# A two-layer hybrid encoder on one NeuronCore: the weight-only steps between the first projection's units stand one unit later

## What is computed

```python
h = layer_norm(x, ln_in_w, ln_in_b)
for l in range(DEPTH):                       # DEPTH = 2
    proj = h @ w_in[l]                       # 1024 -> 3088 columns
    p_ret, p_s5, p_hy, p_ml = split(proj)
    y = concat([retention(p_ret), s5(p_s5, ...), hyena(p_hy, filters), mlstm(p_ml)])
    h = layer_norm(DN_ALPHA * h + y @ w_out[l], ...)
    f = swiglu(h, ...) if l % 2 == 0 else moe_swiglu(h, ...)
    h = layer_norm(DN_ALPHA * h + f, ...)
```

## Time and profile before

| | us |
|---|---|
| median of 3 runs | 1953.71 (1953.68 to 1954.87) |
| the profiled execution, its own time | 1956.23 |
| its span, first to last instruction | 1954.4 |
| PE busy | 1762.7 (90% of the span) |
| DVE busy | 1360.3 (70%) |
| ACT busy | 951.5 (49%) |
| mean granted TensorE clock, share of 2.4 GHz | 0.907 |

### The profile page before, as it was taken

The page is one execution under the profiler, slowest core; times in us unless marked ns, Lnnn a source line. Parts: engine busy times, 40 slices in busy tenths (PEclk is TensorE's granted clock), DMA queues, the critical chain, the costliest instruction groups (busy, mean ns, idle before and its releaser), DMA issues.

```text
span 1954.4 us, 20243 instructions
## 1 busy us (share of the span) xinstructions
PE 1762.7 (90%) x7868; PEld 1396.0 (71%) x7868; DVE 1360.3 (70%) x1437; ACT 951.5 (49%) x951; POOL 54.0 (3%) x33
## 2 busy tenths in 40 slices
PE   6988697999979869789999899899899899998995
PEld 5556575888866658478778678778678687787784
DVE  3449845556621795468878688788688787787886
ACT  1240212445611011266666576666667666666763
POOL 0002100000000110000000000000000000000000
PEclk9996568999989765889999999999899999999997
DMA  9240033434642000748878788788688788787980
GB/s 407 81 172 1 1 133 118 186 138 166 244 193 99 31 1 0 297 182 350 348 284 346 281 343 333 311 348 342 269 350 347 307 341 323 298 347 283 361 324 23
DMA packets 42223, 454.80 MB, mean 233 GB/s; under 512 B 4496, under 2 KB 4624, under 8 KB 9360
## 3 DMA queue, kind: packets, MB, share of 16 engines
q1 hardware_dynamic: 39824, 445.03, 58.2%
q10 hardware_dynamic: 2304, 8.39, 1.1%
HBM read 443.96 MB, written 9.44 MB: 232 GB/s over the span
## 4 chain that ended last, share of the span: by engine, by line
PE 81%; DVE 11%; ACT 3%; issue 2%; DMA 2%; SPq 0%; DVEq 0%; POOL 0%; PEldq 0%
PE bank L908 30%; PE bank L928 15%; PE bank L818 6%; PE bank L543 4%; PE bank L552 4%; PE bank L749 3%; PE bank L827 3%; DVE ring_lo L1566 2%; PE bank L873 2%; PE bank L710 2%; PE bank L892 2%; ACT ex_up_hi L1105 2%; PE bank L683 1%; DMA cst<-const 1%; PE bank L916 1%
## 5 line engine op out<-in xcount | busy, mean ns | idle before, releaser
L1566 DVE TENSOR_TENSOR ring_lo<-ring,ex_up_hi 128x2048 fp32r<-128x2048 f32 x226 | 517.4, 2290 | 125.9 <-ACT ex_up_hi L1105 125.9
L1105 ACT ACTIVATE ex_up_hi<-ring 128x2048 fp32r<-128x2048 f32 x226 | 432.7, 1915 | 181.5 <-PE bank L908 167.8
L908 PE MATMUL bank<-ex_up_hi,ex_x_hi 128*128 128x512 f32 x896 | 371.4, 414 | 14.2 <-DVE ring_lo L1566 13.5
L908 PE MATMUL bank<-ring_lo,ex_x_hi 128*128 128x512 f32 x896 | 353.4, 394 | 5.8 <-issue 5.8
L908 PE MATMUL bank<-ex_up_hi,ex_x_lo 128*128 128x512 f32 x896 | 352.6, 394 | 0.0
L1686 DVE TENSOR_TENSOR ring_lo<-ring,ex_w_hi 128x2048 fp32r<-128x2048 f32 x112 | 255.6, 2282 | 0.0
L908 PEld LDWEIGHTS bank<-ex_up_hi,ex_x_hi 128*128 128x128 f32 x896 | 169.2, 189 | 63.3 <-DVE ring_lo L1566 19.6
L1190 ACT ACTIVATE ex_w_hi<-ring 128x2048 fp32r<-128x2048 f32 x112 | 213.2, 1904 | 0.0
L928 PE MATMUL bank<-ex_w_hi,ex_mid_hi 128*128 128x512 f32 x448 | 182.1, 407 | 34.3 <-DVE ex_mid_lo L1680 34.3
L908 PEld LDWEIGHTS bank<-ring_lo,ex_x_hi 128*128 128x128 f32 x896 | 168.7, 188 | 38.3
L908 PEld LDWEIGHTS bank<-ex_up_hi,ex_x_lo 128*128 128x128 f32 x896 | 169.3, 189 | 35.8 <-issue 3.8
(11 more groups left out here) (317 smaller groups left out, 2356.3 us busy)
## 6 DMA issues: line engine op xcount, KB each, us to landing
ring<-moe SPq DMA_DIRECT2D x113, 2048.0 KB, 7.7
ring<-moe SPq DMA_DIRECT2D x112, 1024.0 KB, 7.6
ring<-ffn SPq DMA_DIRECT2D x11, 3072.0 KB, 11.1
ring<-w_in SPq DMA_DIRECT2D x8, 3072.0 KB, 16.1
ring<-w_out SPq DMA_DIRECT2D x4, 2048.0 KB, 8.3
tab<-yT ACTq DMA_DIRECT2D x16, 512.0 KB, 2.7
ring<-tab SPq DMA_DIRECT2D x2, 3072.0 KB, 10.3
lnb<-ln SPq DMA_DIRECT2D x5, 1024.0 KB, 6.9
```

Of the source, the lines that this page charges most:

```text
L908: ins = mm(b[:, :], ex_x[j][x_][:, k, :], (ex_up_hi, lo)[w_][:, k, :], start=(k == 0 and m == 0), stop=(k == KT - 1 and m == 2))
L1105: act(ex_up_hi[:, HS * q:HS * (q + 1), :], wt[:, HS * q:HS * (q + 1), :], ACT.Copy).then_inc(e_uh, 1)
L1566: tt(ring_lo[s][:, half], ring[s][:, half], hi.bitcast(F32), ALU.subtract).then_inc(e_ul, 1)
```

## The change

The rows of `BESIDE` change, and nothing else:

```diff
-        BESIDE = [(0,), (1,), (2, 3), (4, 5, 6), (7, 8, 9), (10, 11), (12, 13), (14, 15), (16, 17), (18, 19), (20,),
+        BESIDE = [(), (0,), (1, 2), (3, 4, 5), (6, 7, 8), (9, 10), (11, 12), (13, 14), (15, 16), (17, 18), (19, 20),
                   (), ()]
```

## The result

The change makes the kernel slower: 1968.05 us median against 1956.35 (six runs each), ratio 1.0058, interval 1.0044 to 1.0072. That is 11.7 us where the forecast said 7.7. The time lies outside the stated range of 1956.0 to 1966.0. Two things make up the miss of 6.6 us against 1961.4: before itself has a median of 1956.35 in six runs, 2.6 above the 1953.71 of three on which the forecast was put, and the change costs 4.0 more than forecast. Taken as differences from 1953.71, the ends of the range are +2.3 and +12.3, and 11.7 lies near the upper one.

The account below looks back on a forecast made before the run. The last table store was taken to set the mixers' start, any shift reaching the end. Part 1's +2.1 and part 2's +5.6 gave +7.7 us on the median 1953.71, so 1961.4 us, range 1956.0 to 1966.0.

Parts of the forecast that it names:

- part 1: PE up to the end of unit 6: removed and added waits and slow clock balance to +2.1 us (-2.0 to +4.3).
- part 2: From unit 6 to the last table store: DVE row and two more tables make the load's issue 5.6 us later.
- The first rival, ACT drained in time: Behind unit 6: ACT again waits for unit 10, only one more table counts (2.82 us); 1958.6 us, chance 0.12.
- the second, waits that cost no clock: PE's new waits bring no slow clock: part 1 is -2.0, total +3.6 us, 1957.3, within 0.2%; chance 0.1.
- The faster one: Mixers get a better clock through their later start: -9.1 us, 1944.6, if the mean rose to 0.75; chance 0.05.
- The rival with all costs at their upper ends: Whole kernel: +4.3 + 5.6 + 2.1 = +12.0 us, 1965.7; chance 0.12.
- Unit 1 no longer stands behind the constants: PE at unit 1 and step 0: 3.36 idle, 2.25 and 0.44 slow clock removed, together 6.05 us gained.
- Step 2 behind step 1: PE waits for step 1's sine: 4.7 us idle plus 2.25 slow clock, 6.95 added.
- Step 5 behind step 3: PE waits for step 3's window product on DVE: 1.5 us idle added, clock cost taken as 0.
- Step 7 behind step 6: PE waits for DVE's four L1273: 1.9 us idle plus 1.80 slow clock, 3.7 added.
- Removed ahead of step 6: PE's old wait for step 5's window product goes: 2.21 us idle and 1.80 slow clock, 4.01 gained.
- 2.1 us for the mixers: Starting the mixers at another moment may move them by about 2.1 us either way.

Follow-up runs that it names:

- e4: Kernel before with step 20 alone moved one unit earlier, so all eight tables stand ahead of unit 10's reading out; ratio 0.9988, 2.2 us faster.
- e8: Kernel before with filler steps reordered: step 0 behind unit 1, dependent steps apart, step 11 early, all tables ahead of unit 10; ratio 0.9938, 1941.03 us.
- e2: Kernel before with the change's second half alone (steps 11 to 20 as in the change); ratio 1.0007, 1.4 us slower.
- e5: The unedited change again, beside new runs of before; ratio 1.0073, 14.3 us slower.
- e6: The change plus six unused matmuls of constants in two of PE's new waits (ahead of steps 2 and 5); ratio to before 0.9997.
- f1: Kernel before, unedited, profiled a second time; 1961.5 us.
- f3: Kernel before, unedited, profiled a third time; 1955.3 us.
- d04 to d16: Kernel before with 4, 8, 12 or 16 chained DVE products ahead of layer 0's first mixer tile; ratios to before 1.0003, 1.0019, 1.0032, 1.0040.
- e1: Kernel before with the change's first half alone (steps 0 to 10 as in the change, 11 to 20 as before); ratio 0.9999.
- f2: The kernel of e1 profiled a second time, no further edit; 1957.6 us.
- f4: The kernel of e1 profiled a third time, no further edit; 1967.4 us.
- e3: Kernel before with step 2 alone moved right behind step 1, after unit 1; ratio 1.0044, 8.6 us slower.
- e7: Kernel before with no step behind unit 0, early steps one unit later, dependent ones mostly apart, 12 to 20 unchanged; ratio 0.9975, 5.2 us faster.

## Why the prediction was wrong

The steps that failed are two terms of part 1: the 6.05 us to be gained at the constants, which is 4.1, and the 0 us of slow clock behind step 5's wait, which is 1.8 with its matmul. Together they are 3.8 of the 5.0 us by which part 1 came out dearer than the 2.1 forecast. The kinds of cost (waits, and slow matmuls behind them) and part 2 were right.

**Read right.** The mixers' start hangs on the last table store (e4, e8). Behind unit 6 the row of rotation, step 11, step 12 and rotation puts the first table 14.8 us behind it, ACT no longer waits for unit 10, and two tables follow it: +5.7 measured in after, e2, e5 and e6, +5.6 forecast. The first rival, ACT drained in time, is out, and so is the second, waits that cost no clock. The faster one is out too: both kernels' mixers lie between 168 and 173 us. The rival with all costs at their upper ends (1965.7) comes nearest to the time, but not by its terms: part 1 is above its upper end, and the mixers in after gave nothing (168.4 against 170.1).

**Wrong: part 1, "+2.1 us at the end of unit 6".** Nine executions with before's order up to unit 6 (before, f1, f3, e2, e4, d04 to d16) have the rotation at 88.6 to 92.9, mean 90.5. Five with the change's order (after, e5, e1, f2, f4) have it at 96.0 to 98.2, mean 97.6. The part costs 7.1 us, above the upper end of 4.3 that I gave it. The one profile that I read has the latest rotation of the nine, and against it alone the cost is 4.8. With 5.7 the 7.1 makes 12.8, against 11.7 and 14.3 measured. So the milestones account for the whole change, and for e3; they don't for e1, e2, e6 and the delays, as said above. Term by term:

- *"Unit 1 no longer stands behind the constants: together 6.05."* Measured 4.1: unit 1 ends at 35.0 to 38.3 in before's order (mean 35.9), at 30.9 to 33.3 in the other (mean 31.8). This is the first failing step. I took both ends of the price from one execution, and it was among the dearest of the nine. PE's timeline in f3, before's order, shows the usual case (six of the nine have unit 1 end between 35.0 and 35.4):

```profile
16.90 9.63 PE L543 MATMUL bank<-hT,ring 128*128 128x256 f32 x32 [0.69 <-ACT hT L978]
27.31 0.61 PE L495 MATMUL bank<-cst,pr 33*64 33x256 f32 x2 [0.78 <-DMA cst<-const]
27.85 7.17 PE L543 MATMUL bank<-hT,ring 128*128 128x256 f32 x32
```

  Here unit 0 is slow (9.63), the wait only 0.78, and unit 1 fast. In the profile of before unit 0 was fast, the wait 3.36 and unit 1 slow. The wait for the constants hides a slow start of unit 0, since they land near 27.3 in any case (step 0 begins at 27.2 to 27.6 in all nine); the change pays a slow start in full (33.1 in after against 30.9 in e1). In none of the nine are both slow: six have unit 0 at 8.9 to 9.65 and unit 1 at 7.17, three the reverse. I counted the slow unit 1 as always there and the slow unit 0 as never.
- *Step 2 behind step 1, 6.95.* Measured 4.92 of idle, 1.09 in the first L506 and 1.6 to 2.3 in unit 3: 8.0 on the mean of five. The slow clock of the L506 itself (2.07 against 1.12 in e6) was left out.
- *Step 5 behind step 3, "I take 0" for the clock.* This is the second failing step: after 1.6 us without work unit 4 took 8.86 in all five executions. Measured 1.61 + 0.14 + 1.69 = 3.4 for 1.5 (0.14 is what the matmul takes more by itself than as half of the four rows).
- *Step 7 behind step 6, 3.7.* Measured 2.14 of idle and a slow clock in two of five (5.4 for 3.7): 2.9.
- *Removed ahead of step 6, 4.01.* The 2.21 of idle are in all nine; the L513 behind it took 3.70 in four and 5.1 to 6.5 in five, 4.7 on the mean: 3.3.

Summed: 8.0 + 3.4 + 2.9 - 4.1 - 3.3 = 6.9, against the 7.1 of the rotations.

The page's rule that the number of slow matmuls differs from run to run (the Trainium skill, TensorE: Matmul & The Clock Gate, part 1) describes these executions. I had cited it and drawn nothing from it for the sum, beyond the spread of 1.2 us in three runs; some 90 executions of before ranged from 1948.9 to 1961.5.

**The range.** It allowed 2.1 us for the mixers. The stretch behind L1501, whose instructions never change, took from 1798 to 1810 us in the profiles here. A range from one profile was too narrow for that alone. It was also put on the median of three runs, and three more moved that by 2.6 us.

## What to carry to other kernels

When weight-only steps are laid between units as filler, look for the DVE or ACT result that each step's matmul reads: here a whole unit between covered most of them (e7, e8), while two dependent steps behind one unit turned their latency into idle time of PE, and in most profiles the matmuls behind it ran slow as well. Watch as well what a step's shift does to the last thing in the row that someone waits for: here eight table stores, which gained by starting early and lost by the instructions set ahead of them. Whether such a shift comes out whole at the end is another matter: here a bare delay of 5.8 us cost 3.7. And price a wait that ends on a DMA landing by its end, not by its length: what stands in front of it is free as long as it ends before the landing. Take such a price from several executions.

## What the runs showed of the hardware that was not expected

- An idle stretch of 1.6 us on PE was followed by slow matmuls in five of five profiles, one of 2.1 us in three of six and one of 2.2 us in seven of eleven (granted clock 0.50 where slow, as in after from 63 to 65 us). The length of the gap alone doesn't tell: the 2.1 us gap had a slow group behind it in e6, where the two gaps before it were filled, and none in after.
- The first unit took 8.9 to 9.65 us in some executions and 7.17 in others, with the same instructions in front of it. From 17 to 19 us PE has 5 rows of it in f3 where before has 11, as at half clock, yet the windows give the granted clock as 1.00 in both. So that the clock makes this unit slow is read from the lengths of its matmuls and not shown by that column (first line before, second f3):

```profile
17.00:19.00 2.00, 2.00 (x11) 1.74 (x11) 0.00 (x0) 0.00 (x0) 0.00 (x0) 1.00 0.96 407
17.00:19.00 2.00, 2.00 (x5) 1.64 (x6) 0.00 (x0) 0.00 (x0) 0.00 (x0) 1.00 1.05 443
```

- Identical instructions from L1501 to the last norm took between 1798 and 1810 us; between e1 and f4, PE was busy 13.6 us longer in the three stretches above. A comparison's interval can be narrower than what the next one gives: e1's order took 1953.9 to 1958.4 in eleven executions, and 1957.6 and 1967.4 in two taken later.
